# A hybrid encoder layer in float32 on one core: conditioning rows summed by TensorE, a third weight panel in its own place, VectorE's sums moved ahead of its low parts

## The chip, the cores and the metric

The kernel runs on one core of one Trainium2 chip. The metric is the device time in microseconds (us). Each figure of it below is the median of several runs; lower is better.

## What is computed

One layer of an encoder over 512 tokens with a model width of 1024, everything in float32. It has two sub-layers, each with an adaptive norm: the root-mean-square norm of `x` is scaled and shifted per column by values that come from a conditioning vector `c`.

```
c_act = silu(c)
ada = c_act @ ada_w + ada_b                     # 1024 x 6144
shift1, scale1, gate1, shift2, scale2, gate2 = split(ada, 6)
h = rms_norm(x, norm_mix_w) * (1 + scale1) + shift1
u = h @ w_in                                    # 1024 x 8448: attention, HGRN2, RWKV-7, gates
merged = g_a * (o_a @ w_a) + g_b * (o_b @ w_b) + g_c * (o_c @ w_c)
x = x + gate1 * (merged @ w_out)
h = rms_norm(x, norm_ffn_w) * (1 + scale2) + shift2
x = x + gate2 * ((silu(gate_h) * up_h) @ ffn_w_out)
```

Nothing of `h` exists before `shift1` and `scale1`, and those need eight panels of `ada_w` (1 MB each) to be loaded and multiplied by `c_act`. The change is all in this first part, up to the seven RWKV panels of `w_in`.

## The kernel before

**Panels.** Weights come in panels of 1024 x 256 float32 values (1 MB, [128, 2048] in SBUF), in the order of `panel_stream`, all issued by the SyncE queue (SP). The first eight conditioning panels (f = 0 to 7; even f is a quarter of shift1, odd f the same quarter of scale1) go to the six places `cond0` to `cond5`; f = 6 and 7 reuse the first two when those are read. All other panels go through three places of `raw`. The order at the start is f0, f1, RWKV panel 0, f2, f3, RWKV panel 1, f4 to f7, RWKV panel 2, two more conditioning panels, RWKV panel 3, two more, and so on.

**Two parts of each number.** A float32 product is made of three passes of float32r: ScalarE rounds a panel into `whi` (`split_hi`), VectorE writes the rest into `wlo` (`take_panel`), and TensorE multiplies hi by hi, lo by hi and hi by lo (`split3`). There are two places for a split panel (`RING`), so ScalarE rounds panel m when panel m-2 has been multiplied. `h` is kept as `hhi` and `hlo` in eight blocks kc of 128 columns, each made by `first_h` (ScalarE) and `first_low` (VectorE).

**Conditioning, quarter q = 0 to 3** (blocks 2q and 2q+1 of `h`). The scale panel is summed over its rows by TensorE: `scale(q)`, 8 products with `ca_wide` (`c_act`, 32 columns wide), then ScalarE copies the result to `ada_acc` (`scale_row`). The shift panel is summed by VectorE: `ada_sum`, 8 instructions of 128x256 into two accumulators. TensorE then turns both into columns with one-column products, `ada(q)` (four, for two accumulators) and `ada(4+q)` (two). VectorE adds the bias (`ada_out`) and forms the factor `gmul` (`conditioned`); only then can `first_h` run. ScalarE also normalises the four token blocks of `x` (`norm_root`, `norm_scaled`), and `transposes` turns two blocks of columns at a time.

**TensorE's queue at the start** is written by hand: `scale`, `ada`, `transposes` of the quarters in turn, and from the second quarter on parts of the first two RWKV panels between them (`unit_part`: per block kc six products of 128x512). After that the loop over n = 2 to 6 takes a whole RWKV panel (two units of 24 products) and the `ada` products of two later conditioning panels.

**VectorE's and ScalarE's loop over n = 0 to 6** evicts the two units of panel n with the token shift (`u_prev` by ScalarE, then `R`, `K`, `V` by VectorE). Ahead of the eviction, for n above 0, stands the split of the panel n+1 and, inside `take_panel`, `ada_sum` of the two conditioning panels that follow it (`late_sum`). `s_panel_taken` counts both kinds; SP issues the load of a streamed panel when the one three places before it is taken, and TensorE's `next_panel` waits for it too.

Of the kernel before, what the change touches and what calls it, by code (L numbers as in the profile page):

```python
# [22 lines left out]
F32R = mybir.dt.float32r  # L23
U8 = mybir.dt.uint8
I32 = mybir.dt.int32
ALU = mybir.AluOpType
# [3 lines left out]
P = 128  # L30
# [168 lines left out]
def bank_plan():  # L199
# [179 lines left out]
def build(nc, x, ada_w, w_in, wba, wbb, wbc, w_out, f_in, f_out, w2, a2, g2,  # L379
# [3 lines left out]
    with ExitStack() as ctx:  # L383
# [42 lines left out]
        cond = [at(f"cond{n}", 48 + 8 * n, [P, KC, 256]) for n in range(COND)]  # L426
        lev_f32 = at("lev_f32", 40, [P, 2 * RW_LEVELS + 1, 64])
# [99 lines left out]
        s_shift_sum = sem("shift_sum")  # L527
# [52 lines left out]
        s_normed = sem("normed")  # L580
        s_panel_hi = sem("panel_hi")
# [82 lines left out]
        hi_slots = [whi[:, 0, :], whi[:, 1, :], spare_hi[:, :], last_hi, up_hi[:, :]]  # L664
        lo_slots = [wlo[:, 0, :], wlo[:, 1, :], spare_lo[:, :], last_lo, raw_low[:, raw_place(weights[in_place])[0], :]]
# [120 lines left out]
        def _(pool):  # L786
            pool.wait_ge(s_shift_sum, 4)
            pool.wait_ge(*full("scale", 3))
# [70 lines left out]
        def _(act):  # L859
# [105 lines left out]
            scale_row(1)  # L965
# [3 lines left out]
            for q in range(2, 4):  # L969
                scale_row(q)  # L970
                first_h(2 * q)
                first_h(2 * q + 1)

            for n in range(7):
                if n:
                    split_hi()
# [382 lines left out]
        def _(dve):  # L1359
# [14 lines left out]
            def ada_sum(n, i):  # L1374
# [4 lines left out]
                for k in range(KC):  # L1379
# [8 lines left out]
                    else:  # L1388
                        dve.wait_ge(s_ada_step, step)
                        done = s_shift_sum if n < 4 else s_panel_taken  # L1390
                        stt(acc, src[:, k, :], ca[:, k:k + 1], acc, ALU.mult, ALU.add).then_inc(done, 1)
                        dve.wait_ge(done, up(done))
# [15 lines left out]
            def take_panel():  # L1408
# [3 lines left out]
                if m >= len(weights):  # L1412
                    return
# [6 lines left out]
                dve.wait_ge(s_panel_taken, up(s_panel_taken))  # L1420
                while i + 1 < len(panels) and panels[i + 1][0] == "ada":
                    i += 1
                    late_sum(i)

# [70 lines left out]
            ada_sum(0, first_at[0])  # L1495
# [4 lines left out]
            ada_sum(1, first_at[2])  # L1500
# [4 lines left out]
            ada_sum(2, first_at[4])  # L1505
            conditioned(2)
            ada_sum(3, first_at[6])
# [6 lines left out]
            first_low(7)  # L1514

            dve.wait_ge(s_constants_late, 16)
            dve.wait_ge(s_masks, 1)
            for n in range(7):
                if n:
                    take_panel()  # L1520
# [8 lines left out]
                for k in range(sum(LATE_WITH[:n]), sum(LATE_WITH[:n + 1])):  # L1529
                    ada_out(ADA[8 + k])  # L1530

# [507 lines left out]
        def _(pe):  # L2039
# [66 lines left out]
            def ada(n):  # L2106

                if n < 4:
                    pe.wait_ge(s_shift_sum, n + 1)
                elif n < 8:  # L2110
                    pe.wait_ge(*freed("scale", n - 4))
# [4 lines left out]
                parts = 1 if 4 <= n < 8 else 2  # L2116
# [13 lines left out]
            def transposes(kcs):  # L2130
                pe.wait_ge(s_normed, TB)
# [6 lines left out]
            def second_transposes(q, kcs):  # L2138
                pe.wait_ge(s_normed, TB + 2 * q + 2)
# [35 lines left out]
            def scale(q):  # L2175

                src = loaded(pe, first_at[2 * q + 1]).rearrange("p (k n) -> p k n", k=KC)
                ps = begin("scale", q)
# [3 lines left out]
                end(last, "scale", q)  # L2182
# [12 lines left out]
            scale(0)  # L2195
# [3 lines left out]
            scale(1)  # L2199
# [3 lines left out]
            units = [[begin("rw", 2 * n + m) for m in range(2)] for n in range(2)]  # L2203
            first = [next_panel()]
            unit_part(first[0], 0, units[0], (0, 1))
            first.append(next_panel())
            unit_part(first[1], 1, units[1], (0, 1))
            unit_part(first[0], 0, units[0], (2, 3))
            scale(2)
            transposes((4, 5))  # L2210
            ada(2)
            ada(6)
            unit_part(first[1], 1, units[1], (2, 3))
            scale(3)
            transposes((6, 7))
            ada(3)
            unit_part(first[0], 0, units[0], (4, 5))
            ada(7)
            unit_part(first[0], 0, units[0], (6, 7))
            unit_part(first[1], 1, units[1], (4, 5))  # L2220
# [505 lines left out]
```

## Time and profile before

| | |
|---|---|
| median of 3 runs | 1179.01 us (1178.69 to 1179.12) |
| the profiled execution's own time | 1174.85 us |
| its span, first to last instruction | 1173.0 us |
| TensorE (PE) busy | 1103.3 us, 94% |
| VectorE (DVE) busy | 622.8 us, 53% |
| ScalarE (ACT) busy | 472.3 us, 40% |
| mean granted TensorE clock | 0.984 |

Times in the trace are microseconds from the span's start. PE is the matrix product, PEld the load of its weights, SPq the issue of a DMA by SyncE. The granted clock is a share of full speed: 1.00 is 2.4 GHz, 0.50 is 1.2 GHz, and a stretch between shows a mean. The durations of matrix products overlap, so the pitch from one start to the next is what counts.

### The profile page before, as it was taken

How to read it: one execution, taken by the hardware profiler on the slowest of the kernel's cores; microseconds unless marked ns; L12 is line 12 of the kernel's file. 1: busy time of each engine (PE TensorE's matmuls, PEld its weight loads, DVE VectorE, ACT ScalarE, POOL GpSimd, SP SyncE). 2: the span in 40 equal slices, each digit the busy share in tenths (PEclk: the TensorE clock that was granted, in tenths of full speed). 3: DMA queues.
4: the chain of work that ended last, by engine and by line, in shares of the span. 5: the costliest groups of instructions: out<-in, count | busy, mean ns of one | idle time of the engine just before them, and what ended most of it. 6: DMA issues, size and time to landing. Idle time of an engine off the chain costs nothing.

```text
span 1173.0 us, 18368 instructions
## 1 busy us (share of the span) xinstructions
PE 1103.3 (94%) x7721; PEld 893.3 (76%) x7721; DVE 622.8 (53%) x861; ACT 472.3 (40%) x589; POOL 25.9 (2%) x45
## 2 busy tenths in 40 slices
PE   3999999988999998889998999999999999999997
PEld 2788657778887677778776777888888888878885
DVE  4477766354543444884864638765345423333346
ACT  7332542233232347565655666446121221222333
POOL 0100000100000000001100010000000000000000
PEclk9999989999999899899999999999999999999999
DMA  9867513311010722216732148430535323223211
GB/s 343 274 206 241 172 63 108 114 56 47 12 48 26 264 90 74 69 47 210 265 101 71 46 146 313 168 108 18 174 114 168 126 101 108 79 101 107 72 36 72
DMA packets 106778, 145.44 MB, mean 124 GB/s; under 512 B 3252, under 2 KB 86440, under 8 KB 106696
## 3 DMA queue, kind: packets, MB, share of 16 engines
q1 hardware_dynamic: 93544, 109.25, 28.2%
q0 software_dynamic: 5664, 21.38, 5.4%
q10 hardware_dynamic: 7488, 13.63, 3.1%
q8 instruction: 61, 1.00, 0.4%
q14 instruction: 21, 0.17, 0.1%
HBM read 128.53 MB, written 15.73 MB: 123 GB/s over the span
## 4 chain that ended last, share of the span: by engine, by line
PE 80%; DVE 8%; ACT 8%; issue 2%; DMA 1%; ACTq 0%; SPq 0%; DVEq 0%
PE bank L2059 79%; DVE wlo L1364 1%; DMA cond<-in_ada_w 1%; ACT whi L874 1%; ACT gate_row L889 1%; ACT LX L1042 1%; DVE SC L1364 0%; DVE mg L1364 0%; ACT L1276 0%; DVE Z L1364 0%; DVE ang L1367 0%; PE bank L2574 0%; ACT probT L1260 0%; ACT KBtok L1048 0%; DVE bonus L1558 0%
## 5 line engine op out<-in xcount | busy, mean ns | idle before, releaser
L2059 PE MATMUL bank<-hhi,whi 128*128 128x512 f32 (+1 forms) x816 | 328.7, 403 | 9.0 <-DVE wlo L1364 3.9
L2059 PE MATMUL bank<-hlo,whi 128*128 128x512 f32 (+1 forms) x816 | 319.0, 391 | 0.0
L2059 PE MATMUL bank<-hhi,wlo 128*128 128x512 f32 (+1 forms) x816 | 318.9, 391 | 0.0
L1364 DVE TENSOR_TENSOR wlo<-raw,whi 128x2048 fp32r<-128x2048 f32 (+1 forms) x79 | 168.3, 2131 | 257.0 <-ACT whi L874 256.1
L874 ACT ACTIVATE whi<-raw 128x2048 fp32r<-128x2048 f32 (+1 forms) x79 | 141.1, 1786 | 216.3 <-PE bank L2059 184.6
L2059 PEld LDWEIGHTS bank<-hhi,whi 128*128 128x128 f32 x816 | 156.5, 192 | 50.3 <-issue 6.6
L2059 PEld LDWEIGHTS bank<-hhi,wlo 128*128 128x128 f32 x816 | 155.9, 191 | 32.7
L2059 PEld LDWEIGHTS bank<-hlo,whi 128*128 128x128 f32 x816 | 156.7, 192 | 30.3 <-issue 0.5
L2059 PE MATMUL bank<-whi,d_hi 128*128 128x512 f32 x160 | 63.2, 395 | 1.2 <-DVE hid L1364 1.2
L2059 PE MATMUL bank<-whi,d_lo 128*128 128x512 f32 x160 | 63.1, 395 | 0.0
L2059 PE MATMUL bank<-wlo,d_hi 128*128 128x512 f32 x160 | 63.1, 394 | 0.0
L889 ACT ACTIVATE gate_row<-bank 128x512 f32<-128x512 f32 x52 | 31.1, 599 | 47.8 <-PE bank L2059 44.7
L1331 ACT ACTIVATE f_tmp<-bank 128x512 f32<-128x512 f32 x22 | 13.2, 598 | 92.3 <-PE bank L2059 92.2
L1042 ACT ACTIVATE LX<-bank 128x512 f32<-128x512 f32 x20 | 12.0, 598 | 72.7 <-PE bank L2059 72.6
L1367 DVE SCALAR_TENSOR_TENSOR ada_acc<-raw,ca,ada_acc 128x256 f32<-128x256 f32 x96 | 40.8, 480 | 0.6
L2059 PEld LDWEIGHTS bank<-whi,d_hi 128*128 128x128 f32 x160 | 30.1, 188 | 8.6 <-issue 1.5
L2059 PEld LDWEIGHTS bank<-whi,d_lo 128*128 128x128 f32 x160 | 30.1, 188 | 7.0
L2059 PEld LDWEIGHTS bank<-wlo,d_hi 128*128 128x128 f32 x160 | 30.1, 188 | 7.0
L1664 DVE COPY_PREDICATED X<-lev,bank 128x512 f32<-128x512 uint8 x16 | 11.7, 730 | 43.4 <-PE bank L2059 43.4
L1364 DVE TENSOR_TENSOR hid<-f_tmp,bank 128x512 f32<-128x512 f32 x22 | 15.1, 687 | 34.5 <-PE bank L2059 34.2
L1668 DVE COPY_PREDICATED XT<-lev,bank 128x512 f32<-128x512 uint8 x20 | 14.7, 737 | 20.5 <-PE bank L2059 20.5
L2059 PE MATMUL bank<-whi,hhi 128*128 128x512 f32 x64 | 25.4, 397 | 0.0
(351 smaller groups left out, 1589.0 us busy)
## 6 DMA issues: line engine op xcount, KB each, us to landing
raw<-in_w_in SPq DMA_DIRECT2D x33, 1024.0 KB, 5.6
raw<-in_f_in SPq DMA_DIRECT2D x22, 1024.0 KB, 5.0
raw<-in_ada_w SPq DMA_DIRECT2D x16, 1024.0 KB, 5.2
early_out<-gate_row ACTq DMA_DIRECT2D x52, 256.0 KB, 2.1
raw<-in_f_out SPq DMA_DIRECT2D x11, 1024.0 KB, 4.9
cond<-in_ada_w SPq DMA_DIRECT2D x8, 1024.0 KB, 10.8
sg<-early_out POOLq DMA_DIRECT2D x4, 1536.0 KB, 10.8
raw<-in_w_out SPq DMA_DIRECT2D x4, 1024.0 KB, 5.1
```

Of the source, the lines that this page charges most:

```text
L874: do(hi_slots[slots[m]][:, 0:src.shape[1]], src, ACT.Copy).then_inc(s_panel_hi, 1)
L889: do(stage[:, u % 2, :], bank_of("early", u)[:, :], ACT.Copy).then_inc(free_sem("early", u), 1)
L1042: do(LX[:, :, :], by_chunk(bank_of("rw t", n, i)[:, :]), ACT.Copy).then_inc(free_sem("rw t", n, i), 1)
L1331: do(f_tmp[:, m, :], ps[:, :], ACT.Sigmoid).then_inc(s_ffn_sig, 1)
L1364: return v.tensor_tensor(out_, a, b, op)
L1367: return v.scalar_tensor_tensor(out=out_, in0=a, scalar=s_, in1=b, op0=op0, op1=op1)
L1664: v.copy_predicated(X[:, :, :], lmask(i, 0), by_chunk(bank_of("rw p", n, i)[:, :]))\
L1668: v.copy_predicated(XT[n % 2][:, :, :], lmask(i, 1), by_chunk(bank_of("rw pt", n, i)[:, :]))\
L2059: return t.matmul(out_, lhsT, rhs, start=start, stop=stop, skip_group_check=True)
```

## The change

1. `scale(q)` becomes `row(f)` for all eight panels: TensorE sums the shift panels as well, ScalarE copies each row to `ada_acc[:, f % 2]`, and `ada(n)` for n below 8 has one accumulator (two products in place of four for the shift quarters). VectorE's four `ada_sum` calls go.
2. VectorE, not ScalarE, scales the normalised `x`.
3. TensorE's hand-written order: the pieces of RWKV panels 0 and 1 stand differently between the conditioning quarters, and the last quarter's conditioning stands ahead of blocks 4 to 7 of both panels.
4. RWKV panel 2 gets a place of its own (`third_hi`, `third_lo`, over `cond4` and `cond5`) and is split before the loop over n.
5. In that loop VectorE first evicts the two units of panel n, then sums two conditioning panels, then takes the low part of panel n+3. ScalarE's split moves one panel on in the same way.

```diff
-    own = {total - spare: RING, total - spare + 2: RING + 2, total - 1: RING + 1}
+    own = {2: RING + 2, total - spare: RING, total - spare + 2: RING + 3, total - 1: RING + 1}
...
-        b.add("scale", q)
+        b.add("row", 2 * q)
+        b.add("row", 2 * q + 1)
...
         def cond_released(eng, f):
-            if f % 2:
-                eng.wait_ge(*full("scale", f // 2))
-            else:
-                eng.wait_ge(s_shift_sum, f // 2 + 1)
+            eng.wait_ge(*full("row", f))
...
-            def scale_row(q):
-                act.wait_ge(*full("scale", q))
-                if q:
-                    act.wait_ge(*full("ada", 4 + q - 1))
-                do(ada_acc[:, 1, 0, :], bank_of("scale", q)[:, 0:256], ACT.Copy).then_inc(free_sem("scale", q), 1)
-                act.wait_ge(*freed("scale", q))
+            def row(f):
+                act.wait_ge(*full("row", f))
+                if f >= 2:
+                    act.wait_ge(*full("ada", ADA[f - 2]))
+                do(ada_acc[:, f % 2, 0, :], bank_of("row", f)[:, 0:256], ACT.Copy).then_inc(free_sem("row", f), 1)
+                act.wait_ge(*freed("row", f))
...
-            for tb in range(TB):
-                norm_scaled(0, tb, x_in, x_norm)
-            scale_row(0)
+            row(0)
+            row(1)
             split_hi()
             first_h(0)
             first_h(1)
...
+            row(6)
+            row(7)
+            split_hi()
+            first_h(6)
+            first_h(7)
             for n in range(7):
-                if n:
+                if 0 < n < 6:
                     split_hi()
...
             for tb in range(TB):
                 row_rstd(0, tb)
-            ada_sum(0, first_at[0])
+                ts(x_norm[:, tb, :], x_in[:, tb, :], col(RSTD + tb), ALU.mult).then_inc(s_x_normed, 1)
+                dve.wait_ge(s_x_normed, up(s_x_normed))
             conditioned(0)
             take_panel()
             first_low(0)
             first_low(1)
-            ada_sum(1, first_at[2])
...
             first_low(6)
             first_low(7)
+            take_low()
...
             for n in range(7):
-                if n:
-                    take_panel()
...
                 for k in range(sum(LATE_WITH[:n]), sum(LATE_WITH[:n + 1])):
                     ada_out(ADA[8 + k])
+                if n < 5:
+                    sums_behind(weights[n + 2])
+                    take_low()
...
-                parts = 1 if 4 <= n < 8 else 2
+                parts = 1 if n < 8 else 2
```

TensorE's queue at the start, before. `cond_55` and `cond_57` are the scale panels f1 and f3, `cst,ada_acc` are the one-column products, `cst,x_norm` the transposes, and the last row begins block 0 of RWKV panel 0.

```order
L2059 MATMUL bank<-cond_55,ca_wide 32x256 x8
L2059 MATMUL bank<-cst,ada_acc 128x1 x6
L2135 MATMUL bank<-cst,x_norm 128x128 x8
L2059 MATMUL bank<-cond_57,ca_wide 32x256 x8
L2135 MATMUL bank<-cst,x_norm 128x128 x8
L2059 MATMUL bank<-cst,ada_acc 128x1 x6
L2059 MATMUL bank<-hhi,whi 128x512
```

The same place after the change.

```order
L2070 MATMUL bank<-cond_54,ca_wide 32x256 x8
L2070 MATMUL bank<-cond_55,ca_wide 32x256 x8
L2070 MATMUL bank<-cst,ada_acc 128x1 x4
L2144 MATMUL bank<-cst,x_norm 128x128 x8
L2070 MATMUL bank<-cond_56,ca_wide 32x256 x8
L2070 MATMUL bank<-cond_57,ca_wide 32x256 x8
L2144 MATMUL bank<-cst,x_norm 128x128 x8
L2070 MATMUL bank<-cst,ada_acc 128x1 x4
L2070 MATMUL bank<-hhi,whi 128x512
```

Two groups of eight row products more stand ahead of the first product of `h`, and the one-column products are 4 and 4 in place of 6 and 6.

VectorE's queue from the end of the conditioning to the second panel of its loop, before. `R` is the eviction of two units, `ada_acc` are two sums of conditioning panels.

```order
L1364 TENSOR_TENSOR hlo<-h_tmp,hhi 128x512 x2
L1367 SCALAR_TENSOR_TENSOR R<-bank,small,u_prev 128x512 x2
L1364 TENSOR_TENSOR wlo<-raw,whi 128x2048
L1371 TENSOR_SCALAR ada_acc<-raw,ca 128x256 x2
L1367 SCALAR_TENSOR_TENSOR ada_acc<-raw,ca,ada_acc 128x256 x6
L1371 TENSOR_SCALAR ada_acc<-raw,ca 128x256 x2
L1367 SCALAR_TENSOR_TENSOR ada_acc<-raw,ca,ada_acc 128x256 x6
L1367 SCALAR_TENSOR_TENSOR R<-bank,small,u_prev 128x512 x2
L1364 TENSOR_TENSOR wlo<-raw,whi 128x2048
```

The same place after the change.

```order
L1368 TENSOR_TENSOR third_lo<-raw,third_hi 128x2048
L1371 SCALAR_TENSOR_TENSOR R<-bank,small,u_prev 128x512 x2
L1375 TENSOR_SCALAR ada_acc<-raw,ca 128x256 x2
L1371 SCALAR_TENSOR_TENSOR ada_acc<-raw,ca,ada_acc 128x256 x6
L1375 TENSOR_SCALAR ada_acc<-raw,ca 128x256 x2
L1371 SCALAR_TENSOR_TENSOR ada_acc<-raw,ca,ada_acc 128x256 x6
L1368 TENSOR_TENSOR wlo<-raw,whi 128x2048
L1371 SCALAR_TENSOR_TENSOR R<-bank,small,u_prev 128x512 x2
```

The low part of panel 2 stands ahead of the first eviction, and that of panel 3 ahead of the second.

## Rows read from the trace of the kernel before

**Rows 1.** The page, busy time of each engine (share of the span) and instructions.
```profile
PE 1103.3 (94%) x7721; PEld 893.3 (76%) x7721; DVE 622.8 (53%) x861; ACT 472.3 (40%) x589; POOL 25.9 (2%) x45
```

**Rows 2.** Waits of TensorE, whole span: us in total, times, longest.
```profile
PE bank L2059 <- DVE hlo L1364: 3.4, 2, 2.8
```

**Rows 3.** Timeline of TensorE, 12 to 31 us: start, duration, instruction, idle before.
```profile
15.75 1.94 PE L2059 MATMUL bank<-cond,ca_wide 128*32 128x256 f32 x16 [11.84 <-DMA cond<-in_ada_w]
17.62 2.72 PE L2059 MATMUL bank<-cst,ada_acc 128*128 128x1 f32 x12
20.20 1.95 PE L2135 MATMUL bank<-cst,x_norm 128*128 128x128 f32 x8
23.86 1.93 PE L2059 MATMUL bank<-cond,ca_wide 128*32 128x256 f32 x16 [1.71 <-DMA cond<-in_ada_w]
25.72 1.97 PE L2135 MATMUL bank<-cst,x_norm 128*128 128x128 f32 x8
28.33 2.72 PE L2059 MATMUL bank<-cst,ada_acc 128*128 128x1 f32 x12 [0.64 <-DVE ada_acc L1367]
30.91 0.77 PE L2059 MATMUL bank<-hhi,whi 128*128 128x512 f32 x1
```

**Rows 4.** Timeline of TensorE, 35 to 66 us.
```profile
35.32 0.44 PE L2059 MATMUL bank<-hlo,whi 128*128 128x512 f32 x1
...
41.06 0.39 PE L2059 MATMUL bank<-hhi,wlo 128*128 128x512 f32 x1
41.38 1.07 PE L2059 MATMUL bank<-cond,ca_wide 128*32 128x256 f32 x16
42.38 1.09 PE L2135 MATMUL bank<-cst,x_norm 128*128 128x128 f32 x8
43.31 1.40 PE L2059 MATMUL bank<-cst,ada_acc 128*128 128x1 f32 x12
44.57 0.48 PE L2059 MATMUL bank<-hhi,whi 128*128 128x512 f32 x1
...
49.41 0.95 PE L2059 MATMUL bank<-cst,ada_acc 128*128 128x1 f32 x8
50.22 0.48 PE L2059 MATMUL bank<-hhi,whi 128*128 128x512 f32 x1
50.53 0.39 PE L2059 MATMUL bank<-hlo,whi 128*128 128x512 f32 x1
...
52.80 0.39 PE L2059 MATMUL bank<-hhi,wlo 128*128 128x512 f32 x1
53.03 0.50 PE L2059 MATMUL bank<-cst,ada_acc 128*128 128x1 f32 x4
56.37 0.80 PE L2059 MATMUL bank<-hhi,whi 128*128 128x512 f32 x1 [2.83 <-DVE hlo L1364]
...
59.09 0.50 PE L2059 MATMUL bank<-hhi,whi 128*128 128x512 f32 x1
...
66.03 0.46 PE L2059 MATMUL bank<-hhi,whi 128*128 128x512 f32 x1
```

**Rows 5.** Windows: busy us of each engine (instructions), then clock, DMA share, GB/s.
```profile
54.00:57.00 3.00, 0.64 (x2) 0.54 (x3) 0.75 (x2) 2.81 (x4) 0.87 (x1) 0.81 0.99 320
```

**Rows 6.** SP's issues, then issues of 10.2 to 12 us with time to landing.
```profile
10.30 5.32 SPq L768 DMA_DIRECT2D cond<-in_ada_w  x2
...
29.48 2.63 SPq L777 DMA_DIRECT2D raw<-in_w_in  x1
...
cond<-in_ada_w SPq DMA_DIRECT2D x1, 1024.0 KB, 10.8
```

**Rows 7.** Timelines of ScalarE and VectorE, 61 to 87 us.
```profile
61.59 1.92 ACT L874 ACTIVATE whi<-raw 128x2048 fp32r<-128x2048 f32 x1
...
78.08 0.62 DVE L1371 TENSOR_SCALAR ada_acc<-raw,ca 128x256 f32<-128x256 f32 x2 [1.95 <-PE bank L2059]
78.61 2.58 DVE L1367 SCALAR_TENSOR_TENSOR ada_acc<-raw,ca,ada_acc 128x256 f32<-128x256 f32 x6
...
86.35 2.29 DVE L1364 TENSOR_TENSOR wlo<-raw,whi 128x2048 fp32r<-128x2048 f32 x1
```

More of the change, by code:

```diff
@@ L426, in build @@
         cond = [at(f"cond{n}", 48 + 8 * n, [P, KC, 256]) for n in range(COND)]
+        third_hi = at("third_hi", 80, [P, 2048], F32R)
+        third_lo = at("third_lo", 88, [P, 2048], F32R)
         lev_f32 = at("lev_f32", 40, [P, 2 * RW_LEVELS + 1, 64])
@@ L580, in build @@
         s_normed = sem("normed")
+        s_x_normed = sem("x_normed")
         s_panel_hi = sem("panel_hi")
@@ L663, in build @@
         in_place = own_panel()
[L664 to L665 removed]
+        hi_slots = [whi[:, 0, :], whi[:, 1, :], spare_hi[:, :], last_hi, third_hi[:, :], up_hi[:, :]]
+        lo_slots = [wlo[:, 0, :], wlo[:, 1, :], spare_lo[:, :], last_lo, third_lo[:, :], raw_low[:, raw_place(weights[in_place])[0], :]]
         def cond_released(eng, f):
[L669 to L672 removed]
+            eng.wait_ge(*full("row", f))
         def slot_released(eng, m):
@@ L786, in _ @@
         def _(pool):
-            pool.wait_ge(s_shift_sum, 4)
-            pool.wait_ge(*full("scale", 3))
+            pool.wait_ge(*full("row", 7))
             pool.dma_start(cst[:, N_FIRST:NCONST], consts[:, N_FIRST:NCONST]).then_inc(s_constants_late, 16)
@@ L964, in _ @@
             first_h(1)
-            scale_row(1)
+            row(2)
+            row(3)
             split_hi()
@@ L968, in _ @@
             first_h(3)
[L969 to L972, printed above, removed]
+            row(4)
+            row(5)
+            first_h(4)
+            first_h(5)
+            row(6)
[3 more added lines that the diff above has]
+            first_h(7)
             for n in range(7):
-                if n:
+                if 0 < n < 6:
                     split_hi()
@@ L1389, in ada_sum @@
                         dve.wait_ge(s_ada_step, step)
-                        done = s_shift_sum if n < 4 else s_panel_taken
-                        stt(acc, src[:, k, :], ca[:, k:k + 1], acc, ALU.mult, ALU.add).then_inc(done, 1)
-                        dve.wait_ge(done, up(done))
+                        stt(acc, src[:, k, :], ca[:, k:k + 1], acc, ALU.mult, ALU.add).then_inc(s_panel_taken, 1)
+                        dve.wait_ge(s_panel_taken, up(s_panel_taken))
             def ada_out(n):
@@ L1423, in take_panel @@
                     late_sum(i)
+            def take_panel():
+                m = split_next[0]
+                if m < len(weights):
+                    take_low()
+                    sums_behind(weights[m])
             def late_sum(i):
@@ L2106, in ada @@
             def ada(n):
[L2108 to L2111, printed above, removed]
+                if n < 8:
+                    pe.wait_ge(*freed("row", ADA.index(n)))
                 else:
@@ L2173, in _, with row @@
             pe.wait_ge(s_ca_wide, 1)
-            def scale(q):
-                src = loaded(pe, first_at[2 * q + 1]).rearrange("p (k n) -> p k n", k=KC)
-                ps = begin("scale", q)
+            def row(f):
+                src = loaded(pe, first_at[f]).rearrange("p (k n) -> p k n", k=KC)
+                ps = begin("row", f)
                 for k in range(KC):
@@ L2181, in scale @@
                     last = mm(ps[rows, 0:256], ca_wide[:, k, :], src[:, k, :], k < 4, k >= KC - 4)
-                end(last, "scale", q)
+                end(last, "row", f)
             def unit_part(slot, n, tiles, kcs):
@@ L2193, in unit_part @@
                             end(last, "rw", 2 * n + m)
-            scale(0)
+            row(0)
+            row(1)
             ada(0)
@@ L2198, in _ @@
             transposes((0, 1))
-            scale(1)
+            units = [[begin("rw", 2 * n + m) for m in range(2)] for n in range(2)]
+            row(2)
+            row(3)
             transposes((2, 3))
@@ L2202, in _ @@
             ada(5)
-            units = [[begin("rw", 2 * n + m) for m in range(2)] for n in range(2)]
             first = [next_panel()]
             unit_part(first[0], 0, units[0], (0, 1))
+            row(4)
             first.append(next_panel())
             unit_part(first[1], 1, units[1], (0, 1))
-            unit_part(first[0], 0, units[0], (2, 3))
-            scale(2)
+            row(5)
             transposes((4, 5))
@@ L2212, in _ @@
             ada(6)
+            unit_part(first[0], 0, units[0], (2, 3))
             unit_part(first[1], 1, units[1], (2, 3))
-            scale(3)
+            row(6)
+            row(7)
             transposes((6, 7))
             ada(3)
+            ada(7)
             unit_part(first[0], 0, units[0], (4, 5))
-            ada(7)
+            unit_part(first[1], 1, units[1], (4, 5))
             unit_part(first[0], 0, units[0], (6, 7))
-            unit_part(first[1], 1, units[1], (4, 5))
             unit_part(first[1], 1, units[1], (6, 7))
```

13 lines of the change are left out of this document (5 added, 8 removed).

## The prediction

> **What bounds the kernel now.** I read the page first: TensorE is busy 94% of the span, VectorE 53%, ScalarE 40% [rows 1]. So a change of this kind can only give what TensorE loses in idle time, at the low clock, or in work that is added or dropped. The chain that ended last runs through TensorE nearly throughout, so time won early should stay won unless a later step is held by something else. The waits of TensorE over the whole span show one item in the changed part that is not a load: 3.4 us on `hlo`, one wait of 2.8 [rows 2]. Then I read TensorE's timeline where the change works.
>
> Up to 30.91 us nothing of `h @ w_in` runs [rows 3]. The order there is: the row sum of f1 at 15.75 when its load lands, six one-column products, transposes, the row sum of f3 at 23.86 when that load lands, transposes, then 0.64 us idle because VectorE's sum of f2 ends only at 28.3, and six one-column products from 28.33. The first product of the RWKV panels starts at 30.91. From there to 66.03, where panel 2 begins, the 96 products of panels 0 and 1 (128x512) take 35.1 us [rows 4]. Their warm pitch is (52.80 - 50.53) / 10 = 0.227 us, so 96 would need 21.8. The rest of it is: the low clock from 30.91 to 35.3, where the duration falls from 0.63 to 0.39 (half of 4.4 us, 2.2); conditioning groups (41.06 to 44.57, the like at 47.5 to 50.2, and 53.03 to 53.5); an idle 2.84 before 56.37, as the last quarter's `h` comes right after its conditioning; and the low clock again, which the windows show as a granted mean of 0.81 in 54 to 57 [rows 5]: the clock fell to 1.2 GHz after that idle time, and six products took 56.37 to 59.09. From 66.03 to 135 TensorE's timeline has no gap of note.
>
> **The change part by part.**
>
> *Start of the products.* The row products take a pitch of 17.62 - 15.75 = 1.87 at the low clock, transposes 1.86, six one-column products 30.91 - 28.33 = 2.58, so four take 1.72 [rows 3]. The load of f0 had landed by the time VectorE began to sum it, before 14 us, so `row(0)` fits ahead of f1's landing at 15.7 at a cost of nothing: TensorE was idle there for 11.84 us. `row(1)` then ends at 17.6; the four one-column products end at 19.4 and transposes at 21.2. f2 was issued at 10.30 and landed 10.8 later, at 21.1 [rows 6], so `row(2)` runs from 21.2 to 23.1, in what was idle time (1.71 before 23.86). `row(3)` starts at 23.86 as before. Transposes run 25.7 to 27.6, four one-column products to 29.3, with no VectorE sum to wait for. **First product at 29.3 instead of 30.91: -1.6.**
>
> The new work that the trace does not show is VectorE's scaling of `x`, 128x1024 four times. Two instructions of 128x256 take 0.62 us [rows 7]. Bounds: no dearer than that width for width, 4 x 1.24 = 5.0 in all, and no cheaper than one such instruction each, 4 x 0.31 = 1.2. Either way it follows the four root steps, and is done by 15 to 16 us, while transposes want it at 19.4; before, they wanted it at 20.20 [rows 3]. Cost nothing; the cover is 3 us.
>
> *Idle and low clock at 53.5 to 59.* The last quarter's conditioning now stands ahead of blocks 4 and 5 of both panels, 24 products or 5.4 us. The chain from the last one-column product through `gmul`, ScalarE and VectorE took 2.84 us [rows 4]. ScalarE's split of panel 2 now stands in this chain (1.92 us [rows 7]), but it starts when `row(7)` is copied, about 1.7 us before the last one-column product ends, so it delays the chain by some 0.3. 5.4 covers 3.2. **Idle time: -2.84.** With it goes the fall of the clock: six products took 2.72 where 6 x 0.227 = 1.36 is warm. **-1.36.** If the cover failed, both would come back.
>
> *Added and dropped TensorE work after 29.3.* Two more groups of row products, 1.00 each at full clock (41.38 to 42.38), one of them breaking the products once more (41.06 to 41.38 is 0.09 over the pitch): +2.09. One-column products: before 6, 4 and 2, for 1.26, 0.81 and 0.5; now 4 and 4 for 1.62: -0.95 [rows 4]. **+1.14.**
>
> *First low clock.* Before, the clock rose 4.4 us after the first product, in the second case 2.7 after it [rows 4]. It cost half of that, 2.2 or 1.4. At worst it rises at the same instant as before, 35.3, which is 6.0 after 29.3 and costs 3.0. I take the nearest row, 4.4, for the same kind of start: 0, with -0.8 and +0.8 as the ends.
>
> *Panel 2 and the loop.* By this sum panel 2 can start at 61.4. Its low part stands behind `hlo` of block 7, which by the chain above is written by about 55; 2.29 more is 57.4 [rows 7]. Its load was issued at 29.48 and SP's order is the same [rows 6]. Ready with 4 us to spare; before, TensorE did not wait for it either. The early split earns nothing by itself. Panel 3: its load is issued at 57.4 and lands 5 to 6 us later; VectorE meanwhile evicts and makes two sums, 2 x 3.15 us (0.62 + 2.58 less overlap [rows 7]), from 60.5 to 66.8, and takes the low part by 69.1. TensorE wants it at 61.4 + 10.9 + 1.6 = 73.9. For later panels the sums wait for the one-column products of the pair before (as the 1.95 in [rows 7]): 0.9 after a panel ends, then 6.3 and 2.3, so 9.5 after it; the next want is 12.5 after it. 3.0 us of cover, period by period, and VectorE's work of a period (1.5 + 0.4 + 6.3 + 2.3 = 10.5) is under 12.5. Cost nothing. If that cover is gone, TensorE waits once a panel. After the loop each engine has the same order as before, and the shift is kept.
>
> **Sum:** -1.6 - 2.84 - 1.36 + 1.14 = -4.7. The profiled execution took 1174.85 with a span of 1173.0, so its span would be 1168.3. The median of the runs is 4.2 above that execution; the difference is applied to the median: 1179.0 - 4.7 = **1174.3**.
>
> **A rule against it.** The sum rests on f2 being there 2.7 us before f3, as the landings show (21.1 and 23.86 [rows 3, 6]). The Trainium skill (DMA: Bandwidth & Descriptors, Queues, rings and completion order) says that a later transfer of one issuing queue may finish before an earlier one, as nothing orders the 16 engines. By that rule f2 could be usable only with f3. Then two row groups stand behind 23.86, the first product starts at 23.86 + 2 x 1.87 + 1.86 + 1.72 = 31.2, and the sum is -2.8: 1176.2. The trace disagrees here.
>
> **The rivals.**
>
> *The clock takes part of it (1176.5).* It rises at 35.3 as before (+0.8), and the new group of two row sums, transposes and one-column products (2.0 + 0.93 + 0.81 = 3.7 us, against 3.3 and 2.8 before) lets it fall once as at 56 (+1.36): -4.7 + 0.8 + 1.36 = -2.5. For: the group is the longest yet without wide products. Against: the two shorter groups kept the clock at 1.00.
>
> *The transfers land in pairs (1176.2)*, worked out above. Against: each landing seen here is apart from the next.
>
> *The gain is absorbed in the loop (1179).* VectorE's low part now stands behind two sums, which wait for TensorE. If a low part is over 3.0 us later than worked out, TensorE stands still in each of four or five panels; 1 us each is all of 4.7. For: a new order with VectorE 84% busy in the period. Against: the cover.
>
> *Slower (1183.5).* The clock does not rise in the first twelve products but stays at 1.2 GHz through the short pieces. Before, 36 products stood together at that place; now 12 products, a row group, 12, and another group. The work from 33.7 on is 0.4 + 1.1 + 2.7 + 2.8 = 7.0 us at full clock; at half it takes 7.0 more, and with a rise 4.4 into the 24 products behind it 2.2 more again: +9.2, net +4.5. It decides from an extra low-clock stretch of 9.4 us on. Against: twelve slow products last 5.1 us, longer than either rise took, and none of the pieces is idle time.
>
> **How the numbers follow.** Forecast 0.62, the clock 0.16, pairs 0.05, absorbed 0.12, slower 0.05. About 0.2% (2.4 us) is what a measurement of this kernel tells from no change. Faster: all of the forecast, three quarters of the clock case and most of the pairs, 0.78. Same: the rest of them and the absorbed case, 0.17. Slower 0.05. The range leaves out the absorbed and the slower case and holds the others: from 1173.3 (forecast less the 0.8 of an earlier rise, rounded down) to 1177.0 (the clock case and half a microsecond).
>
> **What the profile would show.** First product of the RWKV panels at 29.3, not 30.9; `row(2)` before 23.5; no idle time between the last one-column product and blocks 6 and 7, and a clock of 1.00 in all of 36 to 66; panel 2 at 61.4; no wait for `wlo` up to 135. VectorE's 128x1024 at 0.3 to 1.3 us. I would be wrong by a wait of TensorE for `third_lo`, `wlo` or a bank in the loop, by a low clock in 34 to 51, or by a later stage that does not move forward by the same amount.

## The result, and the profile after the change

| | before | after |
|---|---|---|
| median of 11 runs each | 1175.93 us | 1169.48 us (1166.29 to 1173.81) |
| ratio, 95% interval | | 0.9941 [0.9927, 0.9956] |
| the profiled execution's own time | 1174.85 us | 1168.23 us |
| its span | 1173.0 us | 1166.4 us |
| mean granted clock | 0.984 | 0.984 |

The change makes the kernel 0.59% faster, about 6.9 us (the medians differ by 6.4, the two profiled executions by 6.6). Forecast were 4.7. The three runs shown for the kernel before (1179.01) are among the eleven and lay 3 us above their median (1175.93), so the time forecast, 1174.3, is off by both. All ratios in this document compare fast executions alone; one run of loop_part below, at 2202.71 us, is left out of its ratio.

The page of the kernel after, busy time of each engine, answers to [rows 1]:

```profile
PE 1102.1 (94%) x7769; PEld 889.1 (76%) x7769; DVE 613.9 (53%) x833; ACT 469.3 (40%) x589; POOL 26.0 (2%) x45
```

Its waits of TensorE over the whole span (us in total, times, longest), against [rows 2]. The 2.8 us on `hlo` is gone; the `wlo` group is 0.4 us dearer than before, by a wait that will be seen below:

```profile
PE bank L2070 <- DMA cond<-in_ada_w: 10.8, 3, 9.3
...
PE bank L2070 <- DVE wlo L1368: 5.2, 3, 3.9
...
PE bank L2070 <- DVE hlo L1368: 0.5, 1, 0.5
```

TensorE's timeline of the kernel after, 12 to 70 us, answers to [rows 3] and [rows 4]. In order: rows of f0 and f1, columns, transposes, rows of f2 and f3, transposes, columns, block 0 of panel 0. "Rows" are the products that sum a panel over its rows, "columns" the one-column products. Each product of either kind stands in the trace as two instructions, so the eight products of `row(f)` are x16.

```profile
13.63 1.93 PE L2070 MATMUL bank<-cond,ca_wide 128*32 128x256 f32 x16 [9.34 <-DMA cond<-in_ada_w]
16.29 1.93 PE L2070 MATMUL bank<-cond,ca_wide 128*32 128x256 f32 x16 [0.73 <-DMA cond<-in_ada_w]
18.16 1.87 PE L2070 MATMUL bank<-cst,ada_acc 128*128 128x1 f32 x8
19.88 1.95 PE L2144 MATMUL bank<-cst,x_norm 128*128 128x128 f32 x8
21.76 1.94 PE L2070 MATMUL bank<-cond,ca_wide 128*32 128x256 f32 x16
24.42 1.07 PE L2070 MATMUL bank<-cond,ca_wide 128*32 128x256 f32 x16 [0.73 <-DMA cond<-in_ada_w]
25.43 1.09 PE L2144 MATMUL bank<-cst,x_norm 128*128 128x128 f32 x8
26.36 0.95 PE L2070 MATMUL bank<-cst,ada_acc 128*128 128x1 f32 x8
27.17 0.48 PE L2070 MATMUL bank<-hhi,whi 128*128 128x512 f32 x1
27.48 0.40 PE L2070 MATMUL bank<-hlo,whi 128*128 128x512 f32 x1
...
30.22 1.07 PE L2070 MATMUL bank<-cond,ca_wide 128*32 128x256 f32 x16
31.73 0.50 PE L2070 MATMUL bank<-hhi,whi 128*128 128x512 f32 x1 [0.45 <-DVE wlo L1368]
...
43.09 1.93 PE L2070 MATMUL bank<-cond,ca_wide 128*32 128x256 f32 x32
44.95 1.09 PE L2144 MATMUL bank<-cst,x_norm 128*128 128x128 f32 x8
45.88 0.95 PE L2070 MATMUL bank<-cst,ada_acc 128*128 128x1 f32 x8
46.69 0.48 PE L2070 MATMUL bank<-hhi,whi 128*128 128x512 f32 x1
...
57.71 0.40 PE L2070 MATMUL bank<-hhi,third_hi 128*128 128x512 f32 x1
```

To be seen here: the sixteen instructions of a row take 1.93 us up to f2 and 1.07 for f3. The clock rose between the two, before any product of the RWKV panels; the transposes, the columns and the first product behind it are all short (0.40 where before stood 0.63). The first product starts at 27.17 (before 30.91), panel 2 at 57.71 (before 66.03). Nothing is idle where 2.84 us stood before blocks 6 and 7. The window that answers to [rows 5] shows the clock at 1.00 (each engine's busy us and instructions, then clock, DMA share, GB/s):

```profile
54.00:57.00 3.00, 3.00 (x15) 2.48 (x14) 1.64 (x4) 1.38 (x2) 0.00 (x0) 1.00 0.46 142
```

This column does not show the low clock at the start. In the kernel before it reads 1.00 where ten products of 128x512 took 0.63 us each, as long as they take where it reads 0.50:

```profile
30.00:35.00 5.00, 5.00 (x15) 4.13 (x16) 3.86 (x6) 2.81 (x4) 0.00 (x0) 1.00 1.09 383
```

So each first rise of the clock in this document is read from the durations of instructions, and the mean granted clock, 0.984 in both kernels, says nothing of the gain at the start.

VectorE's timeline shows the operation that the trace before did not have, the low part of panel 2 that is done 3.6 us before panel 2 begins, and its sums in the loop, which start when TensorE has read the sums before them (idle 2.83):

```profile
10.20 0.76 DVE L1375 TENSOR_SCALAR x_norm<-x_in,small 128x1024 f32<-128x1024 f32 x1
...
51.25 2.85 DVE L1368 TENSOR_TENSOR third_lo<-raw,third_hi 128x2048 fp32r<-128x2048 f32 x1
...
69.95 0.62 DVE L1375 TENSOR_SCALAR ada_acc<-raw,ca 128x256 f32<-128x256 f32 x2 [2.83 <-PE bank L2070]
```

**Is the gain kept?** I took the same instruction in both traces. From 121 us (129 before) to 626 us it starts 8.0 to 8.2 us earlier; from 633 us on 6.6 to 6.7 earlier. Between stands this, TensorE's timeline of the kernel after:

```profile
626.13 0.70 PE L2070 MATMUL bank<-qk 64*128 64x256 f32 x4 [3.05 <-ACT prob L1255]
...
628.15 0.63 PE L2070 MATMUL bank<-hlo,whi 128*128 128x512 f32 x1
...
631.13 0.44 PE L2070 MATMUL bank<-hhi,wlo 128*128 128x512 f32 x1
```

and of the kernel before:

```profile
634.33 0.70 PE L2059 MATMUL bank<-qk 64*128 64x256 f32 x4 [3.04 <-ACT prob L1251]
...
635.54 0.40 PE L2059 MATMUL bank<-hlo,whi 128*128 128x512 f32 x1
...
637.87 0.40 PE L2059 MATMUL bank<-hhi,wlo 128*128 128x512 f32 x1
```

Both were idle for the same 3 us. Behind it the clock fell for the eight products at 0.63 in one execution and stayed in the other: 1.5 us. So the changed part won 8.3 us, and of this one execution lost 1.5 elsewhere.

### The profile page after: what moved, and what is told of

Read it like the earlier page. It is cut to its first block, busy times and chain, and to the rows that moved or that the text cites. A ratio compares the mean times of both kernels' runs of the same rounds, so it can differ in the third digit from the quotient of the medians.

```text
span 1166.4 us, 18435 instructions
## 1 busy us (share of the span) xinstructions
PE 1102.1 (94%) x7769; PEld 889.1 (76%) x7769; DVE 613.9 (53%) x833; ACT 469.3 (40%) x589; POOL 26.0 (2%) x45
## 4 chain that ended last, share of the span: by engine, by line
PE 80%; DVE 8%; ACT 7%; issue 2%; SPq 1%; DMA 1%; ACTq 0%; DVEq 0%
PE bank L2070 79%; DVE wlo L1368 1%; ACT whi L873 1%; DMA raw<-in_w_in 1%; SPq L768 1%; ACT gate_row L888 1%; ACT LX L1046 1%; DVE SC L1368 0%; DVE mg L1368 0%; ACT L1280 0%; DVE Z L1368 0%; DVE ang L1371 0%; PE bank L2587 0%; ACT probT L1264 0%; ACT KBtok L1052 0%
## 5 line engine op out<-in xcount | busy, mean ns | idle before, releaser
L2070 PE MATMUL bank<-hhi,whi 128*128 128x512 f32 (+1 forms) x800 | 320.9, 401 | 6.6 <-DVE wlo L1368 4.4
L2070 PE MATMUL bank<-hlo,whi 128*128 128x512 f32 (+1 forms) x800 | 312.3, 390 | 0.0
L2070 PE MATMUL bank<-hhi,wlo 128*128 128x512 f32 (+1 forms) x800 | 311.6, 390 | 0.0
L2070 PEld LDWEIGHTS bank<-hhi,whi 128*128 128x128 f32 x800 | 152.6, 191 | 48.1 <-issue 7.0
L2070 PEld LDWEIGHTS bank<-hhi,wlo 128*128 128x128 f32 x800 | 152.6, 191 | 31.8
L2070 PEld LDWEIGHTS bank<-hlo,whi 128*128 128x128 f32 x800 | 152.7, 191 | 29.2 <-issue 0.5
```

Source lines behind the costliest of these rows:

```text
L2070: return t.matmul(out_, lhsT, rhs, start=start, stop=stop, skip_group_check=True)
```

## The experiments

My theory after the result: the two early losses went as worked out; the rest is the clock, which now rises in the conditioning work since TensorE is busy there, with the wait for VectorE's sum gone and the wait for f3's load cut from 1.71 to 0.73 us. Rivals: ScalarE, freed of scaling `x`, brings `h` sooner; the early split of panel 2 brings it; the runs differ by chance. Each ratio below is to runs of the kernel before that were made beside it.

**cond_part.** Parts 1 to 3 of the change alone.

```diff
-    own = {2: RING + 2, total - spare: RING, total - spare + 2: RING + 3, total - 1: RING + 1}
+    own = {total - spare: RING, total - spare + 2: RING + 2, total - 1: RING + 1}
...
             row(7)
-            split_hi()
...
             first_low(7)
-            take_low()
...
             for n in range(7):
+                if n:
+                    take_panel()
```

> Parts 1 to 3 alone (rows by TensorE, x scaled by VectorE, TensorE's order); panel 2 and the loop as before. If all of the gain lies in the conditioning, as I think: the ratio to the kernel before is that of the whole change within 0.1% (0.994), panel 2 starts near 57.7 us, and TensorE has no wait for wlo up to 135 us. If the early split and the new order of the loop are what carries the gain on: TensorE waits for wlo at panel 2 or in the loop, because VectorE has no room once TensorE is 8 us early, and the ratio is 0.996 to 0.999.

Measured: 0.9975 [0.9955, 0.9996], median 1172.61. The expectation of 0.994 failed, and the other one held. The clock rose at 22.6 us and the first product came at 26.83. At panel 2 its timeline of TensorE has this, and the window the clock of the five us from there:

```profile
60.02 0.71 PE L2067 MATMUL bank<-hhi,whi 128*128 128x512 f32 x1 [2.53 <-DVE wlo L1367]
```
```profile
59.00:64.00 5.00, 3.98 (x11) 3.16 (x11) 4.89 (x12) 0.00 (x0) 0.00 (x0) 0.66 0.57 165
```

The conditioning part starts panel 2 so early that its low part, split in the old place, is late by 2.53 us, and the clock falls behind that idle time. The columns behind panel 2 start at 72.63, against 68.87 with the whole change: 3.8 us. The second run of the whole change, made beside this one (again, below), has a median 3.4 us lower.

**loop_part.** Parts 4 and 5 alone, on the kernel before.

```diff
-    own = {total - spare: RING, total - spare + 2: RING + 2, total - 1: RING + 1}
+    own = {2: RING + 2, total - spare: RING, total - spare + 2: RING + 3, total - 1: RING + 1}
...
+                if n < 5:
+                    sums_behind(weights[n + 2])
+                    take_low()
```

> Parts 4 and 5 alone, conditioning as before. By my sum these change nothing: ratio 1.000 within 0.001, panel 2 starts at 66.0. If they are worth something by themselves: panel 2 or a later one starts earlier, ratio 0.998 or less. ScalarE's split of panel 2 stands ahead of block 6 here, so a loss of up to 2 us is possible if it reaches the chain of the last quarter.

Measured: 1.001 [0.9989, 1.0032]. The clock rose at 35.8, and 2.86 us of idle time stood before block 6, with fourteen slow products behind it:

```profile
56.92 0.80 PE L2073 MATMUL bank<-hhi,whi 128*128 128x512 f32 x1 [2.86 <-DVE hlo L1368]
```

Alone this part gives nothing; beside the conditioning part it takes the ratio from 0.9975 to 0.9941.

**x_by_act.** ScalarE scales `x` again, ahead of `row(0)`.

```diff
             for tb in range(TB):
                 norm_root(0, tb, x_in, x_norm)
+            for tb in range(TB):
+                act.wait_ge(s_rstd, tb + 1)
+                do(x_norm[:, tb, :], x_in[:, tb, :], ACT.Copy, scale=col(RSTD + tb)).then_inc(s_x_normed, 1)
...
-                ts(x_norm[:, tb, :], x_in[:, tb, :], col(RSTD + tb), ALU.mult).then_inc(s_x_normed, 1)
```

> The whole change, but ScalarE scales x again (4.7 us after its root steps). ScalarE then copies row 0 only near 19 us and row 1 after it, so the one-column products, transposes and row 2 start about 1 us later, but row 3 still waits for its load at 24.4. If only the load of f3 sets the start: first product at 27.2 as with the whole change, ratio the same. If the busy stretch of TensorE ahead of row 3 sets the clock: that stretch is moved, and the clock may rise later, first product 27.2 to 29.3 and slow products behind it, 1 to 3 us lost.

Measured: 0.9925 [0.9902, 0.9948]. ScalarE is late for the first columns, but f3's load sets the end; the first product came at 27.22 (27.17 with the change):

```profile
19.54 1.87 PE L2072 MATMUL bank<-cst,ada_acc 128*128 128x1 f32 x8 [1.36 <-ACT ada_acc L922]
...
23.15 2.39 PE L2072 MATMUL bank<-cond,ca_wide 128*32 128x256 f32 x32
```

The rival that frees ScalarE falls: nothing is lost when ScalarE has this work back.

**again.** The changed kernel without any edit, to see what differs between two executions.

> The changed kernel once more, for a second execution in the profile. If the early rise of TensorE's clock (at 24.4 us, in row 3) belongs to the order of the work, it is there again, at the same place within 0.5 us. If it is an accident of when the execution started, the rise comes elsewhere, between 24 and 33 us. The same for the fall at 628 us behind an idle 3.05 us, which the kernel before did not have behind the same idle time: an accident would not stay.

Measured: 0.9946 [0.9927, 0.9964]. Here the clock rose later, at 28.3 us, just after the columns before the first product began. So the instant of the rise does not belong to the order of the work:

```profile
24.44 1.93 PE L2070 MATMUL bank<-cond,ca_wide 128*32 128x256 f32 x16 [0.72 <-DMA cond<-in_ada_w]
26.30 1.97 PE L2144 MATMUL bank<-cst,x_norm 128*128 128x128 f32 x8
28.06 1.05 PE L2070 MATMUL bank<-cst,ada_acc 128*128 128x1 f32 x8
28.98 0.48 PE L2070 MATMUL bank<-hhi,whi 128*128 128x512 f32 x1
```

The start is then near the one forecast (29.3), and still no slow product stands behind it. The instructions from 128 us on are 7.0 earlier than before, and after the idle 3.04 us at 627.19 the clock did not fall.

**before_filled.** The kernel before, with eight products that nothing reads ahead of the rows of f1 and of f3, so that TensorE has as many row products as in the change.

```diff
+            def filler(ps, n):
+                for r in range(n):
+                    for k in range(KC):
+                        rows = slice(32 * (k % 4), 32 * (k % 4) + 32)
+                        mm(ps[rows, 0:256], ca_wide[:, k, :], cst[:, 0:256], k < 4, k >= KC - 4)
...
-            scale(0)
+            scale(0, 1)
...
-            scale(1)
+            scale(1, 1)
```

> The kernel before, with eight extra row products (on constants, their result overwritten by the real ones, so the output does not change) ahead of the sums of f1 and of f3, at the places where the change has rows 0 and 2. All else as before, also VectorE's sums. If it is the busier TensorE ahead of f3's landing that lets the clock rise before the first product, as I now think: the rise comes between 22 and 28.5 us here too, and the products from about 30 us on have no slow ones; 2.2 us less from there plus 1.3 for faster one-column products, ratio 0.997 to 0.998, if the clock does not fall again in between. If the rise came from something else in the change (the four instead of six one-column products, no wait for VectorE): the rise stays near 35 us, ratio 1.000.

Measured: 0.9995 [0.9979, 1.0012]. A miss for my theory as it stood, and the most telling trace:

```profile
25.23 1.09 PE L2135 MATMUL bank<-cst,x_norm 128*128 128x128 f32 x8
27.73 1.93 PE L2059 MATMUL bank<-cst,ada_acc 128*128 128x1 f32 x12 [1.40 <-DVE ada_acc L1367]
29.52 0.77 PE L2059 MATMUL bank<-hhi,whi 128*128 128x512 f32 x1
30.09 0.63 PE L2059 MATMUL bank<-hlo,whi 128*128 128x512 f32 x1
```

The clock did rise, at 25.2 us (transposes at 1.09), then TensorE waited 1.40 us for VectorE's sum, the clock fell while the columns ran, and thirteen products of the panels were slow, to 35.2. A clock that has risen once is in the windows' column too:

```profile
28.50:29.00 0.50, 0.50 (x5) 0.50 (x4) 0.09 (x1) 0.00 (x0) 0.00 (x0) 0.62 1.10 377
```

More work is not enough; this wait must go too.

**before_filled_twice.** The same with eight more such products in that wait.

```diff
-                if n < 4:
+                if n == 1:
+                    filler(begin("ada", 1), 1)
+                    pe.wait_ge(s_shift_sum, n + 1)
+                elif n < 4:
...
```

> The kernel before with the two extra row groups and a third one in the wait of 1.4 us for VectorE's sum of f2 (26.3 to 27.7 us); results of the extra products are overwritten. In the run with two extra groups the clock rose at 25.3 and fell again near 28.5, ahead of the first product. If that idle stretch made it fall: now no slow product behind 29 us, panel 2 about 3 us earlier than before (63.0 to 63.5 at equal loads), ratio 0.997. If one-column products alone let it fall: slow products again, ratio 1.000.

Measured: 0.9982 [0.9966, 0.9997], and 0.47 us of the wait left:

```profile
27.27 1.07 PE L2059 MATMUL bank<-cst,ca_wide 128*32 128x256 f32 x16
28.81 1.50 PE L2059 MATMUL bank<-cst,ada_acc 128*128 128x1 f32 x12 [0.47 <-DVE ada_acc L1367]
30.17 0.48 PE L2059 MATMUL bank<-hhi,whi 128*128 128x512 f32 x1
```

The clock rose at 26.2 us, and no product at the start of the panels is slow. The first one comes 0.74 us earlier than in the kernel before, and panel 2 begins at 63.52 instead of 66.03: 2.5 us by the clock alone, with nothing of the change in it. The six slow products before block 6 are still there.

**late_quarter.** The change with the last quarter's columns behind blocks 4 and 5, as before.

```diff
-            ada(3)
-            ada(7)
             unit_part(first[0], 0, units[0], (4, 5))
             unit_part(first[1], 1, units[1], (4, 5))
+            ada(3)
+            ada(7)
```

> The whole change, but the one-column products of the last quarter stand behind blocks 4 and 5 of both panels again. By my term: TensorE stands idle 2.8 us or more ahead of block 6 (ScalarE's split of panel 2 is done by then), and the clock falls behind it, 1.4 more: 4.2 us slower than the whole change, ratio 0.998 to the kernel before. If the last quarter was covered anyway: no idle time, ratio as the whole change.

Measured: 0.9997 [0.9981, 1.0012]. The idle time is back to the hundredth, and twelve slow products behind it, up to 60.02:

```profile
55.16 0.80 PE L2070 MATMUL bank<-hhi,whi 128*128 128x512 f32 x1 [2.83 <-DVE hlo L1368]
```

Panel 2 begins at 63.17 where it began at 57.71: 5.5 us, of them 2.83 idle and nearly all of the rest the clock. The expected ratio was 0.998, and it came out as if nothing of the change were left. In this profile the start is still 2.7 us earlier than before up to 163 us; then the clock stays low from 163 to 176, where it was low for 6.8 us in the kernel before, and the gain is gone. This later loss is not part of the term.

**pairs.** The change, with the row of f2 held until f3 has landed: the prediction's rival of transfers that land together.

```diff
+            pe.wait_ge(s_cond_in[3], 16)
             row(2)
             row(3)
```

> The whole change, but row 2 waits for the load of f3 as well (the case in which transfers land in pairs). TensorE is idle from 21.8 to 24.4 and then makes both rows. By the sum at the low clock the first product comes 1.9 us later than at the low clock before; if in addition the clock rises only in the products, as it did in the kernel before, the loss against the whole change is 1.9 + 2.6 + 2.2 = up to 6 us (ratio 0.999); if the clock rises in the rows all the same, 1.0 to 1.9 us (ratio 0.995 to 0.996).

Measured: 0.9959 [0.994, 0.9978]; first product at 29.81, none slow. So even then most of the gain would have stood:

```profile
24.02 3.64 PE L2070 MATMUL bank<-cond,ca_wide 128*32 128x256 f32 x32 [2.62 <-DMA cond<-in_ada_w]
27.59 1.57 PE L2144 MATMUL bank<-cst,x_norm 128*128 128x128 f32 x8
```

The transposes, at 1.57 between the two durations seen above (1.09 and 1.97), place the rise at 28.6 us. It came ahead of the first product although TensorE had stood idle for 2.62 us before f3's row, longer than in the kernel before. So that wait alone does not hold the clock down.

**Four kernels on what is left.** Two more places lose the clock: the last LoRA product after 1.56 us of idle time, and the four `rw kn` products (8 rows of weights, two instructions each) after 2.88 idle at 158. In warm_recip twelve products that nothing reads fill the second wait.

```diff
-            pe.wait_ge(s_rw_recip, 1)
             for c in range(4):
                 ps = begin("rw kn", c)
+                if not c:
+                    warm(ps, 12)
+                    pe.wait_ge(s_rw_recip, 1)
```

> The whole change plus twelve 128x512 products on h whose result is overwritten, in TensorE's wait of 2.9 us for VectorE's reciprocal at 155 us; the output does not change. If low-clock stretches behind idle time are what costs beside the idle time: the eight-row products and the panel behind them no longer run slow (5.2 us and nine slow products with the change), 2.5 to 4 us less, ratio to the kernel before 0.991 or less. If the eight-row products themselves let the clock fall: it falls behind them, no gain or under 1 us.

Measured: 0.9927 [0.9903, 0.9951], not told apart from the change. The clock fell in the products of eight rows themselves, at 161.6 us by the windows' column:

```profile
156.27 2.88 PE L2070 MATMUL bank<-hhi 128*128 128x512 f32 x12
159.31 4.95 PE L2070 MATMUL bank<-bonus,cst 8*128 8x512 f32 x8 [0.16 <-DVE bonus L1569]
164.19 0.80 PE L2070 MATMUL bank<-hhi,whi 128*128 128x512 f32 x1
```

split_lora puts half an early unit ahead of the last LoRA product, and split_kn two pieces of 12 products between the `rw kn` ones (`early` takes a range in both).

```diff
+                if c == 3:
+                    early("rw kk", 0, 1)
                 ps = begin("rw a", c)
...
-            early("rw kk")
+            early("rw kk", 1)
```

> The whole change, and half of the following early unit (twelve 128x512 products that are needed anyway) stands ahead of the last of the eight LoRA products, in TensorE's wait of 1.6 us for ScalarE at 131 us. If the idle time and the low clock behind it are both TensorE's loss: 1.6 and 1.2 to 1.7 us gained, ratio to the kernel before 0.991 to 0.992. If VectorE's and ScalarE's chain to the next wait (the reciprocal at 155 us) is what sets the time there, it comes back as a longer wait: no gain.

Measured: 0.9919 [0.9893, 0.9945], span 1164.4. The idle 1.56 and the slow products behind it are gone; ScalarE's squares are now waited for 0.85 us. The next low stretch was longer, 157.5 to 167.7 us (160.2 to 167.0 with the change), and took 1.7 of the 2.0 us back in this execution.

```diff
                 end(mm(ps[:, :], cst[0:8, C_SELT + P * c:C_SELT + P * c + P], bonus[:, :]), "rw kn", c)
-            early(("rw sums", 0))
+                if c in (0, 2):
+                    early(("rw sums", 0), c // 2, c // 2 + 1)
+            early(("rw sums", 0), 2)
```

> The whole change, with the four eight-row products behind the reciprocal (5.2 us in a row, and the clock falls in them) taken apart by two pieces of twelve 128x512 products that follow anyway. If eight-row products in a row let the clock fall: it stays at 2.4 GHz here, 1.5 us less in them and 1.9 less in the nine slow products behind, 3.4 in all, ratio to the kernel before 0.991. If the idle 2.9 us ahead of them is enough to let it fall: it falls as before, no gain. VectorE gets the last of the four about 1 us later, which could eat part of it.

Measured: 0.9915 [0.9884, 0.9947], span 1163.6. The clock fell in the idle 2.88 us, before the first product; this product and nine of the wide ones behind it were slow, and the three other products ran at full clock:

```profile
156.28 2.07 PE L2070 MATMUL bank<-bonus,cst 8*128 8x512 f32 x2 [2.88 <-DVE bonus L1569]
...
163.14 1.98 PE L2070 MATMUL bank<-bonus,cst 8*128 8x512 f32 x4
...
168.01 1.12 PE L2070 MATMUL bank<-bonus,cst 8*128 8x512 f32 x2
```
```profile
155.00:156.00 1.00, 0.00 (x0) 0.00 (x0) 1.00 (x1) 0.54 (x2) 0.00 (x0) 0.80 0.86 314
```

So the expectation's second case holds, and this profile shows no gain by the edit. Against the kernel before, its instructions are 9.98 us earlier at 156 us and 9.48 at 180; with the change they are 8.1 earlier at both. Its span is short since the clock held behind the idle 1.56 at 132 and behind the 3 us at 626, places that the edit does not touch.

best has both edits and `x` scaled by ScalarE.

> Both of these splits on the whole change, with x scaled by ScalarE (whose run had 0.9925). If the three add: 0.9925 less 0.003 and 0.003, ratio 0.987. If only the order at the start carries and the later stage is bound by VectorE: 0.993.

Measured: 0.9886 [0.9866, 0.9905], median 1163.71 (1162.87 to 1164.41), span 1161.8, mean clock 0.988. It beats the kernel before, and its interval lies below that of the change. Which of its three edits brings how much is not resolved: the intervals of the single ones overlap each other and the change's.

## Why the prediction was wrong in size

**The step that failed** is "*First low clock* ... I take the nearest row, 4.4, for the same kind of start: 0, with -0.8 and +0.8 as the ends". It tied the rise to the first product of the panels. The runs showed in its place that the clock rises within the conditioning work, at 22.5 to 28.6 us in all ten profiles of the changed start. So the 2.2 us of slow products went whole, outside both ends given for the term, and no case of the prediction had it. With a row's worth of products in the wait for f3's load, and else the kernel before, the rise comes at 25.2 and 26.2 us, not at 35.3 (before_filled, before_filled_twice). It holds through the first products where VectorE's sum is then waited for 0.47 us, and not where it is 1.40. before_filled_twice shows the clock's part by itself: 0.7 us up to the first product and 1.8 behind it. Filling the wait for f3's load is not enough for the gain (before_filled), and not needed either: in pairs 2.62 us of it stand, with no sum to wait for, and no product was slow. The old start with the sum's wait alone removed was not run.

**The time forecast, 1174.3,** failed by two parts, and each alone puts it outside its range: 4.7 off the median of eleven, 1175.93, is 1171.2, and the measured 6.9 off the median of three, 1179.01, is 1172.1.

**The start, mis-sized.** Forecast -1.6, measured 27.17 - 30.91 = -3.7. Every place in the order is as forecast; against it, f3 was there 0.56 later (24.42 for 23.86; f1 came 0.54 later as well, and so did f3 in loop_part, whose start is the old one, so this is the execution and not the change), and row, transposes and columns took 1.01, 0.93 and 0.81 for 1.87, 1.86 and 1.72: 0.56 - 0.86 - 0.93 - 0.91 = -2.14. This is the clock again, the same failed step. In the second execution (28.98) the start won 1.9 and the slow products 2.2.

**Idle time and low clock before block 6, -2.84 and -1.36.** Right in the profile, and late_quarter gives the converse: with the late columns 2.83 idle returned. The clock's share can be larger than the 1.36 read before: twelve slow products there and fourteen in loop_part, not six.

**Added and dropped work, +1.14.** Right in its parts (1.01, and 43.09 to 44.95 for the pair of rows). It missed 0.45 of wait for `wlo` of panel 1 ("no wait for `wlo` up to 135" was wrong) and 0.2 of slower first products: +1.8. Together -3.7 - 2.2 - 2.84 - 1.36 + 1.8 = -8.3, which is 66.03 - 57.71.

**Panel 2 and the loop.** "The early split earns nothing by itself" is what loop_part shows. But the step counted 4 us of cover for a start at 61.4 and did not ask what the old place of the split would cost once panel 2 starts early. cond_part shows it, 3.8 us. The loop's cover held: no wait of TensorE in the loop, with VectorE's sums waiting 2.1 to 2.8 us for TensorE. "Absorbed in the loop" and "slower" did not come.

**VectorE's scaling of `x`**, bounded between 0.31 and 1.24 and costed at nothing: 0.76 each, done at 15.5, and x_by_act shows no gain by it either.

**The transfers.** f2 was used at 21.76 and f3 at 24.42, apart; the loads landed 2.7 us from one another in every trace here. The rule of the Trainium skill (DMA: Bandwidth & Descriptors, Queues, rings and completion order) says what may happen, and it did not in these runs. Had it, pairs shows 0.9959.

**Later stages "same order, shift kept".** Right up to 626 us, then 1.5 us less in the profiled execution. Two places with the same idle time before and after kept or lost the clock by execution: 3 us at 626 (lost in after, kept in before and again), 1.56 at 132 (lost in before, after and again, kept in cond_part, loop_part and split_kn). A forecast can't have these; they are likely part of why single runs of one kernel lie up to 13 us apart (1169.24 to 1182.48 for 35 runs of the one before).

**The absolute time.** The prediction put the difference onto the median of three runs. That median moved by 3.1 us with more runs, more than the 2.2 us by which the difference was missed.

**Open:** what sets the instant of the rise within 22.5 to 28.6 us, and how much of the gain at the start each of the two waits is worth without the other.

## What to carry to other kernels

Ask of each wait of TensorE in a start-up, however short and however thin the work around it, whether it keeps the clock low: here shortening two such waits was worth more in clock than in time waited (2.1 and 2.2 us against 1.6 in the profiled execution). When a change brings work forward, look up what was ready just in time at the old start, for it is late at the new one. Test the parts of a change each alone: here one gave a quarter of one per cent, the other nothing, and both together 0.6%.

## What the runs showed of the hardware

- The clock rose to 2.4 GHz with no product of 128x512 before it. In the profiles of the changed start it rose during or between the rows (32 columns of weights), transposes or columns (results of one column), at 22.5 to 28.6 us, and in two executions of one kernel between 23.7 and 24.4 and at 28.3. These instants are from durations. The Trainium skill (TensorE: Matmul & The Clock Gate, Part 1) says that the number of slow products at a start varies from run to run of one kernel; the rows agree, 1.93 against 1.07 us for the same sixteen instructions of f3's row.
- Products with eight rows of weights let the clock fall in one profile right behind 2.88 us of back-to-back products and 0.16 idle: the clock fell 2.3 us into them, the eight instructions took 4.95 us, and ten slow wide products followed. That taking them apart helps is not shown: in split_kn four of them took 1.98 at full clock, but the clock had fallen in the idle time before the first and risen again behind it.
- An idle time of 1.40 us was followed by a fall of the clock 0.9 us after its end, with one-column products running (before_filled); 0.47 us at the same place was not (before_filled_twice).
- The same idle time may or may not cost the clock: 3.05 us did in one execution of the changed kernel and 3.04 did not in another.
- VectorE scales 128x1024 float32 by a column in 0.76 us.
